# First attention of a two-block kernel, two heads at a time: paired scores in row tiles, one suffix-sum product for both, values stationary

## The reference

```python
z = einsum('bhtd,bhsd->bhts', q, k) * scale               # scores
log_1m = where(mask, log_sigmoid(-z), 0)                  # mask: s < t
after = cumsum(log_1m, reverse=True) - log_1m             # suffix sums over s
w = where(mask, exp(log_sigmoid(z) + after), 0)
y_a = einsum('bhts,bhsd->bhtd', w, v)
y_a = (y_a * silu(z_a)) @ w_o_sb
```

## Time and profile before

| what | us |
|---|---|
| median of three runs | 1524.81 |
| the profiled execution | 1524.7 |
| its span | 1522.9 |
| TensorE busy | 1071.0 (70%) |
| VectorE busy | 469.0 (31%) |
| ScalarE busy | 174.8 (11%) |
| GpSimd busy | 57.2 (4%) |
| moved by DMA | 506.62 MB, 333 GB/s over the span |

### The profile page before, as it was taken

How to read it: one execution, slowest core, us unless ns; L and a number is a source line. 1 busy time by engine, 2 the same in 40 slices (tenths; PEclk the granted TensorE clock), 3 DMA queues, 4 the chain that set the end, 5 groups by cost and what they waited for, 6 DMA issues and landing times.

```text
span 1522.9 us, 14523 instructions
## 1 busy us (share of the span) xinstructions
PE 1071.0 (70%) x5821; PEld 526.2 (35%) x5821; DVE 469.0 (31%) x948; ACT 174.8 (11%) x412; POOL 57.2 (4%) x86
## 2 busy tenths in 40 slices
PE   5999999997999896645646646646556466466464
PEld 2858555543455553212212212212122122122121
DVE  2255457454246535112112112112122021121121
ACT  0144211102131221000000000000000000000000
POOL 4000211002001000000000000000000000000000
PEclk8999989999998988768978878788788788688688
DMA  9945644657543446999999999999999999999994
GB/s 339 373 164 218 221 154 178 221 150 197 197 163 114 175 165 242 430 427 427 428 428 429 429 428 428 429 429 428 428 429 428 428 429 429 428 429 428 429 428 184
DMA packets 78747, 506.62 MB, mean 333 GB/s; under 512 B 5159, under 2 KB 10559, under 8 KB 54005
## 3 DMA queue, kind: packets, MB, share of 16 engines
q1 hardware_dynamic: 75120, 496.22, 79.5%
q0 software_dynamic: 3520, 9.86, 2.8%
q10 hardware_dynamic: 68, 0.02, 0.0%
HBM read 502.58 MB, written 3.51 MB: 332 GB/s over the span
## 4 chain that ended last, share of the span: by engine, by line
PE 47%; DMA 43%; DVE 6%; SPq 2%; issue 1%; ACT 1%; DVEq 0%
DMA flex<-in_w_dram 37%; PE ps L478 14%; PE ps L942 9%; PE ps L962 6%; DMA arena<-in_w_dram 4%; PE ps L469 4%; DMA ring<-in_w_in_dram 2%; SPq L367 2%; PE ps L920 1%; PE ps L969 1%; DVE arena L1369 1%; DVE mod2p L1418 1%; PE ps L703 1%; DMA x_sb<-in_x_dram 1%; PE ps L434 1%
## 5 line engine op out<-in xcount | busy, mean ns | idle before, releaser
L942 PE MATMUL ps<-ring,arena 128*32 128x512 f32 x1024 | 258.5, 663 | 99.9 <-DMA arena<-in_w_dram 97.7
L942 PE MATMUL ps<-arena 128*32 128x512 f32 x768 | 258.0, 664 | 91.1 <-DMA flex<-in_w_dram 90.0
L478 PE MATMUL ps<-ring,flex 128*128 128x512 f32 (+1 forms) x560 | 251.3, 605 | 6.1 <-DMA ring<-in_w_in_dram 6.1
L962 PE MATMUL ps<-ring,arena 128*32 128x512 f32 x512 | 146.5, 737 | 74.5 <-DMA arena<-in_w_dram 74.5
L962 PE MATMUL ps<-arena 128*32 128x512 f32 x384 | 146.3, 739 | 70.3 <-DMA flex<-in_w_dram 70.3
L478 PEld LDWEIGHTS ps<-ring,flex 128*128 128x128 f32 x560 | 108.9, 199 | 129.3 <-issue 120.9
L942 PEld LDWEIGHTS ps<-ring,arena 128*32 128x32 f32 x1024 | 66.5, 121 | 180.6 <-issue 176.5
L942 PE MATMUL ps<-flex,arena 128*32 128x512 f32 x256 | 128.0, 658 | 0.0
L942 PEld LDWEIGHTS ps<-arena 128*32 128x32 f32 x768 | 60.3, 121 | 169.2 <-issue 164.6
L1890 DVE TENSOR_TENSOR arena<-ps,grow 128x1024 f32<-128x1024 f32 x16 | 19.6, 1224 | 291.0 <-PE ps L962 291.0
L1870 DVE TENSOR_TENSOR arena<-arena,ps 128x512 f32<-128x512 f32 x16 | 11.0, 687 | 241.2 <-PE ps L942 241.2
(11 more groups left out here) (367 smaller groups left out, 1088.8 us busy)
## 6 DMA issues: line engine op xcount, KB each, us to landing
ring<-in_w_dram SPq DMA_DIRECT2D x96, 2048.0 KB, 19.7
arena<-in_w_dram SPq DMA_DIRECT2D x72, 2048.0 KB, 23.8
flex<-in_w_dram SPq DMA_DIRECT2D x24, 2048.0 KB, 28.8
ring<-in_w_ada_dram SPq DMA_DIRECT2D x18, 2048.0 KB, 8.6
ring<-in_w_in_dram SPq DMA_DIRECT2D x17, 2048.0 KB, 10.9
ring<-in_w_out_dram SPq DMA_DIRECT2D x4, 2048.0 KB, 9.7
bias_dram<-arena POOLq DMA_DIRECT2D x1, 2112.0 KB, 45.6
ring<-in_w_o_sb_dram SPq DMA_DIRECT2D x1, 2048.0 KB, 12.5
```

The source lines that it names most:

```text
L478: mm = pe.matmul(ps[:, b, 0:n], lhs3[:, c, i * P:(i + 1) * P], rhs[:, c, :], start=c == 0, stop=c == kc_ - 1)
L942: mm = pe.matmul(ps[32 * e:32 * e + 32, g, :], xe3[:, c, 32 * e:32 * e + 32], mslot(slots[e])[:, c * W5:(c + 1) * W5], start=c == 0, stop= ...
L962: mm = pe.matmul(ps[32 * e:32 * e + 32, 2 + n, :], actT3[:, j, 32 * e:32 * e + 32], mslot(slots[e])[:, o:o + W5], start=j == 0, stop=j == ...
```

## The change

- Heads go in pairs `m` = 0 to 3, at u = 4, 6, 8, 10. The early scores of both heads (2 x 256 columns) share bank 2, the late ones (2 x 128) bank 3.
- `stick_scores(m)` issues four products over 64 rows: early of one head with late of the other on the other half of the rows, then a wait of TensorE on its own `st_half`, then the other two.
- `stick_after(m)` has five products for both heads, and runs in the middle of unit 2m + 6 (`between`); `stick_pv(m)` in the middle of unit 2m + 7. It holds the values (64 columns per head) and moves the weights; head 2m comes out on partitions 0 to 63, head 2m + 1 on 64 to 127, so that features are on partitions.
- The gate `z_a` is computed by `stationary_unit`, features on partitions too. The gated product is written into `qT`, and `y_transposes(0, i)`, its ScalarE copies and their waits fall away.
- VectorE: `stick_split` (four operations) stands where `stick_log` stood; the last operation, over 768 columns, moved behind `mod2_part` of the same `u`. It uses `U` in place of `R`.
- ScalarE: exp and ln over 768 columns; the two exps of `stick_weight(m)` at the top of u = 2m + 6.

```diff
-        def Z(b):
-            return ps[:, 2 + b, 0:384]
+        def early(tile):
+            return tile.rearrange("p (b n) -> p b n", b=2)[:, :, 0:256]
+        def late(tile):
+            return tile.rearrange("p (b n) -> p b n", b=2)[:, :, 256:384]
+        Z_early = ps[:, 2, :].rearrange("p (b n) -> p b n", b=2)
+        Z_late = ps[:, 3, 0:256].rearrange("p (b n) -> p b n", b=2)
         def diag(tile):
...
-            def stationary_unit(n, half, b=None):
+            def stationary_unit(n, half, between=None):
                 b = unit_bank()
                 for m2 in range(2):
+                    if between is not None and m2 == 1:
+                        between()
                     for c in range(DC):
                         mm = pe.matmul(ps[:, b, m2 * 256:(m2 + 1) * 256],
                                        cview(n)[:, c, (2 * half + m2) * P:(2 * half + m2 + 1) * P],
...
+            def token_unit(lhs3, i, rhs, kc_, n=W5, between=None):
                 b = unit_bank()
                 for c in range(kc_):
+                    if between is not None and c == kc_ // 2:
+                        between()
...
+            def stick_scores(m):
+                if m == 0:
                     pe.wait_ge(ld_cst, 16)
                     pe.wait_ge(unit_free[0], 2)
                     pe.wait_ge(unit_free[1], 2)
...
+                else:
+                    pe.wait_ge(st_w, m)
+                kw = dict(stop=False, skip_group_check=True)
+                for first in range(2):
+                    b0, b1 = first, 1 - first
+                    k0, q0 = (a[0][64 * b0:64 * b0 + 64, m, :] for a in (kT3, qT3))
+                    k1, q1 = (a[0][64 * b1:64 * b1 + 64, m, :] for a in (kT3, qT3))
+                    mm = pe.matmul(Z_early[:, b0, :], k0[:, 0:P], q0, start=first == 0, **kw)
+                    mm2 = pe.matmul(Z_late[:, b1, :], k1[:, P:T], q1[:, P:T], start=first == 0, **kw)
+                    if first == 0:
+                        mm.then_inc(st_half, 1)
+                        mm2.then_inc(st_half, 1)
+                        pe.wait_ge(st_half, 2 * m + 2)
+                mm.then_inc(st_z, 1)
+                mm2.then_inc(st_z, 1)
+            def stick_after(m):
+                pe.wait_ge(st_Lm, 2 * m + 2)
+                kw = dict(start=False, skip_group_check=True)
+                never = cc(C_NS)
+                never2 = bass.AP(tensor=never.tensor, offset=never.offset, ap=[never.ap[0], [0, 2], [1, P]])
+                pe.matmul(Z_early, cc(C_GE), early(PT), stop=False, **kw)
+                pe.matmul(Z_late, cc(C_GE), late(PT), stop=False, **kw)
+                pe.matmul(Z_early[:, :, P:256], cc(C_ONE), late(PT), stop=True, **kw)
+                pe.matmul(Z_early[:, :, 0:P], IDN, never2, stop=True, **kw)
+                pe.matmul(Z_late, IDN, never2, stop=True, **kw).then_inc(st_c, 1)
...
+            def pair_pv(w, v, m, start):
+                o = (m % 2) * 256
+                for j in range(2):
+                    for b in range(2):
+                        h = 2 * m + b
+                        mm = pe.matmul(ps[64 * b:64 * b + 64, 5 + m // 2, o + j * P:o + 256], v[:, j, h * HD:(h + 1) * HD],
+                                       w[:, b * 384 + j * 256:b * 384 + 256 + j * P], start=start and j == 0, stop=j == 1,
+                                       skip_group_check=True)
+                return mm
+            def stick_pv(m):
...
+                pe.wait_ge(st_w, m + 1)
+                pair_pv(Pb, v3[0], m, m % 2 == 0).then_inc(st_pv, 1)
...
-                        stationary_unit(n, half)
+                    between = None
+                    if 6 <= u < 14:
+                        between = (lambda: stick_after(u // 2 - 3)) if u % 2 == 0 else (lambda: stick_pv(u // 2 - 3))
+                    if q in (0, 1, 3, 4, 5):
+                        stationary_unit(n, half, between)
                     else:
-                        token_unit(hT3, half, cview(n), DC)
+                        token_unit(hT3, half, cview(n), DC, between=between)
                 if u == 0:
                     pe.wait_ge(ld_small, 16 * 11)
                     f_logits()
...
                     if u == 3:
                         pe.wait_ge(ld_cst, 16)
                     mod2_out(u // 2 - 1)
-                if 0 <= u - 4 < H:
-                    stick_scores(u - 4)
-                if 0 <= u - 5 < H:
-                    stick_after(u - 5)
-                if 0 <= u - 6 < H:
-                    stick_pv(u - 6)
+                if u in (4, 6, 8, 10):
+                    stick_scores(u // 2 - 2)
                 if 0 <= u - 14 < H:
                     fox_scores(u - 14)
                 if 0 <= u - 16 < H:
                     fox_pv(u - 16, fox_tr[u - 16])
-                if u in (14, 15):
-                    y_transposes(0, u - 14)
                 if 0 <= u - 15 < H:
...
             gate_row(0)
-            pe.wait_ge(tr_free, 2)
+            pe.wait_ge(ya_ok, 2)
             chunk_in(WO)
...
+            def stick_soft(m):
+                act.wait_ge(st_zc, m + 1)
+                link(act.activation(zS, zS, ACT.Exp))
+                act.activation(zS, zS, ACT.Ln, bias=1.0).then_inc(st_ln, 1)
+            def stick_weight(m):
+                act.wait_ge(st_c, m + 1)
+                if m:
+                    act.wait_ge(st_pv, m)
+                act.activation(early(Pb), Z_early, ACT.Exp)
+                act.activation(late(Pb), Z_late, ACT.Exp).then_inc(st_w, 1)
...
             for u in range(26):
+                if u in (6, 8, 10, 12):
+                    stick_weight(u // 2 - 3)
                 if u < 24:
...
+            def stick_split(m):
+                dve.wait_ge(st_z, 2 * m + 2)
+                if m:
+                    dve.wait_ge(st_L, m)
+                dve.tensor_scalar(early(zS), Z_early, 40.0, None, ALU.min)
+                dve.tensor_scalar(late(zS), Z_late, 40.0, None, ALU.min).then_inc(st_zc, 1)
+                dve.tensor_scalar(early(U[:]), Z_early, 40.0, -40.0, ALU.max, ALU.add)
+                link(dve.tensor_scalar(late(U[:]), Z_late, 40.0, -40.0, ALU.max, ALU.add))
+            def stick_log(m):
+                dve.wait_ge(st_ln, m + 1)
+                if m:
+                    dve.wait_ge(st_c, m)
+                dve.scalar_tensor_tensor(PT, zS, -1.0, U[:], ALU.mult, ALU.subtract).then_inc(st_L, 1)
...
                         misc[0] += 1
-                if 0 <= u - 4 < H:
-                    stick_log(u - 4)
+                if u in (4, 6, 8, 10):
+                    stick_split(u // 2 - 2)
...
                 if u == 13:
-                    dve.wait_ge(st_pv, 8)
+                    dve.wait_ge(st_pv, 4)
                     dve.wait_ge(unit_free[0], 4)
                     dve.wait_ge(unit_free[1], 4)
-                    for i in range(TI):
-                        dve.tensor_tensor(sz3[0][:, i, :], sz3[0][:, i, :], ps[:, 5 + i, :], ALU.mult).then_inc(ya_ok, 1)
+                    for k in range(2):
+                        cols = slice(k * W5, (k + 1) * W5)
+                        dve.tensor_tensor(qT[0][:, cols], sz[0][:, cols], ps[:, 5 + k, :], ALU.mult).then_inc(ya_ok, 1)
...
                     mod2_part((u - 1) // 2, (u - 1) % 2)
+                if u in (4, 6, 8, 10):
+                    stick_log(u // 2 - 2)
...
-            for h in range(H):
-                pool.wait_ge(st_L, h + 1)
-                below_diagonal(zb(PT, h % 2)).then_inc(st_Lm, 1)
+            for m in range(H // 2):
+                pool.wait_ge(st_L, m + 1)
+                for b in range(2):
+                    below_diagonal(zb(PT, b)).then_inc(st_Lm, 1)
```

More of the change, by code:

```diff
@@ L223, in build @@
             sem(n) for n in ("misc_done", "misc_free", "mod_ok", "mod2_sum", "tr_done", "tr_free", "e_sig")]
-        (st_z, st_zc, st_ln, st_L, st_Lm, st_c, st_w, st_pv) = [
-            sem(n) for n in ("st_z", "st_zc", "st_ln", "st_L", "st_Lm", "st_c", "st_w", "st_pv")]
+        (st_half, st_z, st_zc, st_ln, st_L, st_Lm, st_c, st_w, st_pv) = [
+            sem(n) for n in ("st_half", "st_z", "st_zc", "st_ln", "st_L", "st_Lm", "st_c", "st_w", "st_pv")]
         (fx_u, fx_z, fx_m, fx_p, fx_sc, fx_pv) = [
@@ L562, in fox_scores @@
                     pe.wait_ge(unit_free[1], 6)
-                    pe.wait_ge(st_w, 8)
+                    pe.wait_ge(st_w, 4)
                 if h >= 2:
@@ L1109, in _ @@
                     act.activation(fl[:, 32:48], fl[:, 32:48], ACT.Ln, bias=1.0).then_inc(f_l, 1)
-                if 0 <= u - 4 < H:
[L1111 to L1116, removed]
-                             ps[:, 4, :].rearrange("p (c t) -> p c t", c=4)).then_inc(tr_free, 1)
-                    trs[0] += 1
+                if u in (4, 6, 8, 10):
+                    stick_soft(u // 2 - 2)
                 if 0 <= u - 14 < H:
@@ L1369, in sigmoid_tail @@
                 link(dve.reciprocal(e, e))
-            def stick_log(h):
```

(12 more changed lines are left out.)

19 lines of the change are left out of this document (5 added, 14 removed).

## The result

The changed kernel takes 1513.95 us, the median of four executions (1512.14 to 1517.47), where the kernel before has 1525.84 (1522.19 to 1527.23): ratio 0.9927, 95% interval 0.9905 to 0.9949, so 8 to 14.5 us faster. Six more executions in another group gave 1515.40 (0.9946, 0.9928 to 0.9964), six in a third 1513.68 (0.9921, 0.9907 to 0.9935).

A forecast was written before the change was run, and what follows sets the result against it. The experts' weight DMA was taken to bound the kernel, started earlier by time won in the u loop, through TensorE and, at u = 6 and 7, VectorE. Gains of 2.2, 1.8 and 1.2 us gave 1519.5 us, range 1515.0 to 1525.0.

The forecast's parts named there:

- the transfer rival: At TensorE's 28.87 us wait for a weight chunk, the landing keeps its time and all is lost: 1524.5 us; chance 0.10.
- Suffix sums of a pair: TensorE, both heads' suffix sums in mid unit: 2.61 us where it was 2 x 1.52, without a change of shape.
- Values: TensorE, both heads' value products side by side on two column tiles: 0.98 us where it was 2 x 0.61.
- Scores: TensorE, a pair's scores with late ones hidden and the st_half stop: 1.31 us and 0.2 behind, before 2 x 0.85.
- the sum: Gains on the trace's clock: 2.2, 1.8 and 1.2 us, together 5.2 off the profiled 1524.7, giving 1519.5.
- the serial rival: Tiles run one behind the other, scores 1.75 and values 1.62 us a pair: 1523.1 us; chance 0.16.
- the forecast's two thirds: Of the forecast's chance of 0.45, between 1517.5 and 1521.5 us, two thirds lie below 1520.2 and count as faster.
- the clock rival: TensorE's clock does not fall behind the wait at u = 7: 3.5 us more gain, 1516.0 us; chance 0.20.
- I let the clock fall as before, 1.75 us for `mod2_out` and half speed until 119.0: Behind TensorE's wait at u = 7: unit 8 ends at 126.0 and scores at 127.3, a gain of 2.2 us.
- the transposes of u = 15: Their removal, with the wait for ScalarE's copy, was to gain 1.2 us, between 0.8 and 1.53.
- The clock stays up: Rival: around 110 us mod2_out takes 0.8 and unit 8 its 9.57 us, 3.5 us more, 1516.0; chance 0.20.
- that goes: VectorE's 2.02 us of waiting for ScalarE in each head disappears, because stick_log stands last in u.

The follow-up runs named there:

- e6: Changed kernel with each head's early and late scores one behind the other on the same rows: 1517.14 us, 0.9929 of before.
- e3: Kernel before, plus two unread 512-column products ahead of TensorE's wait at u = 7: 1521.37 us against 1525.72, ratio 0.9976.
- e8: Changed kernel with stick_log directly behind stick_split again, so VectorE waits for ScalarE in place: 1525.07 us, 0.9989 of before.
- e1: Changed kernel with the eight transposes and two ScalarE copies of u = 14 and 15 put back: 1516.45 us.
- e5: Kernel before with only the third operation of the stick logarithm moved behind mod2_part on VectorE: 1518.47 us against 1526.16, ratio 0.9949.
- e4: Changed kernel plus two unread 512-column products ahead of each wait at u = 7 and 15: 1512.55 us, 0.9905 of before.
- e7: Changed kernel with the mod2_part half chunks of u = 6 and 14 moved ahead of split and row maximum: 1508.56 us, 0.9894 of before.
- e10: The changed kernel again, unaltered, on the chip of e7 to e9: 1513.68 us, 0.9921 of before.
- e0: The changed kernel again, unaltered, in another group: 1515.40 us, 0.9946 of before.
- e9: Kernel before, one head at a time, with e5's late last step and e7's early half chunks on VectorE: 1516.64 us.

## Why the prediction was right or wrong

*Right: what bounds the kernel, and that the gain carries through.* Stages behind the loop moved by one amount; the wait for the chunk kept its length but for 1.0 us, so the transfer rival fell.

*Right: the work terms.* Suffix sums of a pair 2.61 foreseen, 2.6 measured. Values 0.98, measured 0.80 and 0.17 on the next unit (3.65 in place of 3.48). Scores 1.31 and 0.2 behind, measured 1.48 and 0.17; inside them the first two products take 0.68 (0.63 foreseen, with the change of shape), the stop on `st_half` shows 0.04 and the second two 0.75, so that the stop costs 0.36 over the 0.43 of bare columns, where the sum had 0.25. Row tiles overlap, so the serial rival fell, by timelines and by e6. The Trainium skill's "TensorE: Matmul & The Clock Gate", Part 3, has row tiles overlap, and the trace agrees, with starts 0.01 us apart. Its semaphore tail would give the two increments ahead of the stop 0.05 us, an estimate from its 26 ns for each. The chain shows 0.04 us as issue, and 0.32 more inside the products behind the stop, so the trace neither bears the tail out nor rules it out. Idle before `mod2_out` of u = 7: 1.7 foreseen, 1.73 measured. From unit 9 to the second attention's scores: 55.66 - 1.8 = 53.9 us foreseen, 184.34 - 130.43 = 53.91 measured. (The chances do not quite add up: the forecast's two thirds and the clock rival give 0.50 for faster, where the text has 0.52.)

*Wrong: the clock in the sum.* The step that failed is "I let the clock fall as before, 1.75 us for `mod2_out` and half speed until 119.0". From the start of `mod2_out` to the end of the scores of u = 8 the sum had 127.3 - 112.1 = 15.2 us; measured 130.43 - 116.70 = 13.7. The clock fell later and for half as long: `mod2_out` and the first microsecond of unit 8 still run at 1.00, and 0.50 lasts from 118.8 to 122.2 us, 3.4 us, where it was 6.9.

```profile
116.70:118.70 2.00, 2.00 (x13) 1.90 (x14) 1.75 (x4) 0.00 (x0) 0.95 (x2) 1.00 0.45 85
119.00:122.00 3.00, 3.00 (x8) 2.36 (x7) 2.96 (x2) 0.00 (x0) 0.00 (x0) 0.50 1.04 401
```

That the wait starts the stretch is shown by e3, where filling it keeps the clock at 1.00 and gains 3.2 us by u = 9. Why it is half as long now stays open. Before, light work stood behind the wait (64-row products, short products bound by their weights), and now a full unit does; but the wait is shorter too, 1.73 us where it was 2.26. No run separates the two. In e8 a full unit stands behind a wait of 4.76 us, and the stretch is as long as before, from 120.8 to 127.5 us:

```profile
121.00:127.00 6.00, 5.17 (x16) 4.57 (x17) 3.87 (x4) 0.00 (x0) 0.00 (x0) 0.50 0.68 234
```
 For the transposes of u = 15 the sum had "1.2 us", below the 1.53 of the chain, because it left the slow stretch its length there as well; from `mod2_out` of u = 15 to that of u = 17 the profiles differ by 27.00 - 22.72 = 4.3. Of this e1 shows 3.8 at that place, but only 2.15 that last to the chunk; and the profile of before has a stretch of 27.0 us there where e3 and e5, with the transposes, have 23.8 and 24.1. Then come 1.6 us at u = 17 to 19, again the clock, and 1.0 us of the chunk's wait, neither in the sum. 1.5 + 3.1 + 1.6 + 1.0 is 7.2; with the 5.2 of the sum that is 12.4, where the profiles differ by 11.55 to the chunk and 1.0 in its wait. What shortened that wait is open.

*Wrong: the weight of the rival.* "The clock stays up" had the mechanism, with a chance of 0.20 and for one place alone. The profiles differ by the clock in three places (behind u = 7, 15 and 17), and the range ended at 1515.0 because one alone was priced. Of the three only the first is shown to follow from the change: at u = 15 filling the wait (e4) or removing it (e7) alters nothing behind it, and the stretch at u = 17 comes and goes between executions of one kernel (e10 against e0). The rows that the rival rested on were also misread: the waits before 225 to 230 and before 250 to 260 us are 0.19 us each, not "of this kind", so the clock fell there with TensorE hardly standing at all.

*Unseen: which part carries the gain.* The prediction led with the pairing, 0.86 us a pair, and told VectorE's new order in a sentence ("that goes"). e8 and e5 turn this round. Without the late step the changed kernel is as slow as before; with it alone the kernel before gains 7.7 us of the 10 to 12 (with both moves, e9, 8.9 of e7's 17.0). The prediction's own rows had it: 2.02 us of standing in each head, on the engine through which the chain runs at u = 6 and 7. A sum that had asked what each part gives without the others would have found it, since 2.2 us of standing for each pair, added to the 1.7 us of idle that it foresaw at u = 7, is a wait of 4 us (e8: 4.76).

*Not settled:* e3's median gains 4.3 us and its profile 8.1 to the chunk. Single executions of before run from 1517 to 1528 us, and only one is profiled, the one with the long stretch at u = 15 to 17. So the 7.0 us that I ascribe to the clock belong to these two profiles. Over executions the medians leave 4.8 to 6.4 us for it: 10.3 to 11.9, less 4.5 of work and 1.0 of the chunk's wait.

## What to carry to other kernels

Where an engine stands in place for another engine's result, move the operation that needs it behind work that is due anyway, and move work that others wait for into the engine's idle time ahead: here both moves took 8.9 us off the median with one head at a time (e9), and up to the chunk 12.5 us, where the pairing on top of them took 4.5. Price a wait on TensorE with what follows it, since the clock can fall behind it and the work there then costs double: the stretch behind the wait of 2.26 us cost 3.2 us more (e3). When a change has several parts, sum each without the others before adding them.

## What the runs showed of the hardware that was not expected

Adding 1.7 us of products whose result nobody reads made the kernel 4.3 us faster (e3), because TensorE's granted clock stayed at 1.00 where it had been 0.50. The clock also falls where TensorE does not stand: in e7 it was busy without a break before and behind `mod2_out` of u = 15, with one-column and other short products, and the clock went to 0.50 from 187.7 to 191.0 us. A half-clock stretch that is avoided at one place can come back a unit or two later: in e10 against e0 the `mod2_out` of u = 17 is 1.68 us later, that of u = 19 0.02, that of u = 21 1.67, and the wait for the chunk 0.04. Two products on different halves of the rows start 0.01 us apart and take 0.68 us together (0.31 + 0.11 + 0.26 in the chain), against 0.86 (0.63 + 0.23) one behind the other in e6's chain.
